# Ten more projection columns by seven block products, in a single-core hybrid decoder step

## What is computed

```python
h = rmsnorm(x, norm1_w)
proj = jnp.einsum('btd,de->bte', h, w_in)
u_pool, u_qkv, b_raw, a_raw, z, gate_pool, gate_delta = jnp.split(proj, SPLITS, axis=-1)
qkv, conv_buf_new = causal_conv(u_qkv, conv_buf, w_conv)
o, s_new = gated_delta_chunked(q, k, v, g, beta, s0, chunk)
o = rmsnorm(o, o_norm_w) * jax.nn.silu(z.reshape(B, T, N_HEADS, HEAD_DV).astype(f32))
merged = jax.nn.sigmoid(gate_pool) * branch_pool + jax.nn.sigmoid(gate_delta) * branch_delta
x = x + jnp.einsum('btd,de->bte', merged, w_out)
```

## Time and profile before

| | |
|---|---|
| median of 3 runs | 602.62 us (601.82 to 602.76) |
| the profiled execution | 602.27 us, its span 600.5 us |
| busy: PE, PEld | 548.7 us (91%), 409.4 us (68%) |
| busy: DVE, ACT, POOL | 270.1, 147.2, 135.2 us |
| HBM | 150.05 MB read, 263 GB/s over the span |

### The profile page before, as it was taken

How to read it: one execution, slowest core, us unless ns; L and a number is a source line. 1 busy time by engine, 2 the same in 40 slices (tenths; PEclk the granted TensorE clock), 3 DMA queues, 4 the chain that set the end, 5 groups by cost and what they waited for, 6 DMA issues and landing times.

```text
span 600.5 us, 12000 instructions
## 1 busy us (share of the span) xinstructions
PE 548.7 (91%) x4820; PEld 409.4 (68%) x4820; DVE 270.1 (45%) x754; ACT 147.2 (25%) x389; POOL 135.2 (23%) x228
## 2 busy tenths in 40 slices
PE   8999999999999999999999999999495959699873
PEld 7899999777877755578889888755262626266431
DVE  4567767755443426146546244651314040414125
ACT  3366465237720002033100133111010101010012
POOL 5777774121200540035004421200000000000000
PEclk9999999999999999999999999999789898999988
DMA  9755444839934273542378944999999999999982
GB/s 242 232 159 151 154 142 141 281 112 332 306 87 134 45 264 110 172 123 89 109 260 350 381 180 199 365 422 420 409 422 419 423 420 419 422 420 419 421 330 79
DMA packets 82582, 158.59 MB, mean 264 GB/s; under 512 B 11245, under 2 KB 65274, under 8 KB 70849
## 3 DMA queue, kind: packets, MB, share of 16 engines
q1 hardware_dynamic: 79724, 154.22, 70.1%
q10 hardware_dynamic: 2805, 3.62, 2.0%
HBM read 150.05 MB, written 7.96 MB: 263 GB/s over the span
## 4 chain that ended last, share of the span: by engine, by line
PE 72%; DMA 23%; DVE 2%; SPq 1%; issue 1%; ACT 1%; DVEq 0%; ACTq 0%
DMA arena<-in_w_up_dram 21%; PE ps L1360 21%; PE ps L1369 13%; PE ps L2013 8%; PE ps L1881 5%; PE ps L1830 3%; PE ps L1784 3%; PE ps L1313 2%; DMA arena<-in_w_in_dram 1%; SPq L582 1%; PE ps L1823 1%; PE ps L2088 1%; PE ps L2068 1%; PE ps L1566 1%; PE ps L1530 1%; PE ps L2025 1%
## 5 line engine op out<-in xcount | busy, mean ns | idle before, releaser
L1360 PE MATMUL ps<-arena 128*128 128x288 f32 x480 | 130.1, 416 | 1.2 <-DMA arena<-in_w_in_dram 1.2
L1360 PEld LDWEIGHTS ps<-arena 128*128 128x128 f32 x480 | 87.3, 190 | 26.8 <-issue 3.1
L2013 PE MATMUL ps<-arena 128*32 128x256 f32 x1024 | 69.3, 433 | 29.0 <-DMA arena<-in_w_up_dram 27.6
L2013 PEld LDWEIGHTS ps<-arena 128*32 128x32 f32 x1024 | 40.1, 124 | 56.7 <-issue 43.2
L1369 PE MATMUL ps<-arena 128*128 128x144 f32 x616 | 78.3, 288 | 0.0
L1369 PEld LDWEIGHTS ps<-arena 128*128 128x128 f32 x616 | 76.3, 190 | 2.5 <-issue 1.9
L2229 DVE SCALAR_TENSOR_TENSOR ps<-arena,ps 128x312 f32<-128x312 f32 x72 | 39.1, 545 | 2.4 <-ACT ps L1021 0.9
L2025 PE MATMUL ps<-arena 128*128 128x128 f32 x336 | 38.7, 276 | 0.0
L2025 PEld LDWEIGHTS ps<-arena 128*128 128x128 f32 x336 | 38.1, 192 | 0.4 <-DVE arena L2898 0.4
L2919 DVE TENSOR_TENSOR arena<-arena,ps 128x256 f32<-128x256 f32 x8 | 3.4, 421 | 66.8 <-issue 36.6
L2088 PE MATMUL ps<-arena 128*128 128x512 f32 x64 | 31.2, 618 | 1.9 <-ACT arena L1258 1.0
(11 more groups left out here) (410 smaller groups left out, 747.3 us busy)
## 6 DMA issues: line engine op xcount, KB each, us to landing
arena<-in_w_up_dram SPq DMA_DIRECT2D x32, 1024.0 KB, 17.3
arena<-in_w_gate_dram SPq DMA_DIRECT2D x28, 1024.0 KB, 18.1
arena<-in_w_down_dram SPq DMA_DIRECT2D x28, 1024.0 KB, 18.6
arena<-in_w_in_dram SPq DMA_DIRECT2D x26, 1024.0 KB, 6.7
out_dram<-arena SPq DMA_DIRECT2D x9, 512.0 KB, 7.6
arena<-in_w_branch_delta_dram SPq DMA_DIRECT2D x4, 1024.0 KB, 6.3
arena<-in_w_out_dram SPq DMA_DIRECT2D x4, 1024.0 KB, 5.4
arena<-in_w_gate_dram SPq DMA_DIRECT2D x8, 512.0 KB, 9.5
```

The lines of the kernel that those rows point to most:

```text
L1360: last = mm(ps[n % 2][:, 0:T], w[:, k, P * (n % 2):P * (n % 2) + P], hT[:, k, :], start=(k == 0), stop=(k == KD - 1))
L2013: last = mm(to[CAP * e:CAP * e + CAP, 0:FE], xgT[u][:, k, CAP * e:CAP * e + CAP], w[e][:, k, :], start=(k == 0), stop=(k == KD - 1))
```

## The change

Items 15 to 19 (z2 to z7, g0 to g3) now go by `fast_pair` too, with banks 0, 1, 3 and 4 (heads keep 5 and 6, samples 7 and 2). Pool makes five more sets of weight sums: those of item 15 ahead of its wait for the convolutions and ahead of the row masks, 16 and 17 ahead of its wait for the zero image's transfer, 18 and 19 around `own_columns`. The slots of items 12 to 23 change from a ring of six to one of four, as slots 4 and 5 hold sums. The heads' buffers `Dt` and `egq` get a second copy each, and a head's decays are made ahead. PE makes one head inside each of the first four pairs and one behind. ACT copies the first product, and applies silu or tanh in three pieces per pair.

```diff
-FAST = range(1, NQKV // 2)
+QKV_FAST = range(1, NQKV // 2)
+Z_FAST = range(15, 20)
+FAST = [*QKV_FAST, *Z_FAST]
-SLOT_OF = [i % 4 if i < NQKV // 2 else i % RA for i in range(A_ITEMS)]
+SLOT_OF = [i % 4 if i < 24 else i % RA for i in range(A_ITEMS)]
...
-DIAG_AT = (N_GATE + 2) // 2 + RA - 1
+DIAG_AT = (N_GATE + 2) // 2 + 3
...
+            sum_weights(15)
             pool.wait_ge(S["conv"], NQKV)
             pool.wait_ge(S["wp_pe"], NG)
...
             nc.gpsimd.memset(XT, 0.0).then_inc(S["memsets"], 1)
+            sum_weights(16)
+            sum_weights(17)
             pool.wait_ge(S["diag"], 16)
             own_columns(0)
+            sum_weights(18)
             pool.wait_ge(S["sd_pe"], 1)
             own_columns(1)
+            sum_weights(19)
...
+            for i in Z_FAST:
+                h = 2 * (i - Z_FAST[0])
+                if 0 < h < H:
+                    rows_exp(h)
+                first_of_pair(i)
+                if h == 0:
+                    rows_exp(0)
+                if h < H:
+                    rows_exp(h + 1)
...
+                pair_curves(i)
...
             pe.wait_ge(S["silu"], 3 * NQKV)
-            for h in range(H):
-                proj(N_Z + Z_AHEAD + h)
-                prep(h)
+            pe.wait_ge(S["wp_ev"], NG)
+
+            def between_pairs(i):
+
+                h = 2 * (i - Z_FAST[0])
+                if h < H:
+                    prep(h)
+                if h == 4:
+                    sample_tiles(2, 0, TS, Nq, lambda own, j: ident[own, own])
+                if h == 6:
+                    sample_tiles(4, 0, TS, IAq, lambda own, j: N2q[own, j, :])
+                if h == H:
+                    state_products(1)
+
+            for i in Z_FAST:
+                h = 2 * (i - Z_FAST[0])
+                fast_pair(i, lambda: between_pairs(i), (ps[0], ps[1], ps[3], ps[4]))
+                if h < H:
+                    prep(h + 1)
...
+            for n in range(2 * Z_FAST[-1] + 2, N_GATE + LEAD_GATES):
                 proj(n)
-                if n == N_GATE + 3:
+                if n == N_GATE + 4:
                     sample_tiles(7, 0, P, TTq, lambda own, j: Rq[own, j, :])
-                if n == N_GATE + 4:
+                if n == N_GATE + 5:
                     sample_tiles(8, 2 * P, P, aqq, lambda own, j: vnq[own, j, :])
```

The additions on DVE (`pair_u2`, `pair_u4`, `pair_u7`, `pair_u5`, `pair_u6`) have this form, and stand among the heads as the third piece of the order below shows:

```diff
+            def pair_u7(i):
+                d0, d1 = pair_rows(i)
+                dve.wait_ge(S["proj"], product(i, P7))
+                dve.wait_ge(S["sums"], added(i, SUM4))
+                V.tensor_tensor(d1[:, HT:T], d1[:, HT:T], ps[4][:, 0:HT], ALU.add).then_inc(S["sums"], 1)
```

More of the change, by code:

```diff
@@ L259, in hybrid_step @@
         kq, vnq = quads(wk.take(2 * P)), quads(wk.take(2 * P))
+        Dts, egqs = (Dt, wk.take(TP)), (egq, wk.take(P))
         vx = rb_room4.rearrange("p (b e) -> p b e", b=BD)
@@ L410, in hybrid_step @@
         for n in range(N_PROJ):
[L411 removed]
+            free[n] = (free[n - 1] if n else 0) + ((3 if n % 2 else 1) if n // 2 in Z_FAST else 1 if n // 2 in FAST else 2 if n < N_POOL else 3 if n < N_Z else 1)
         def chunk(n):
@@ L775, in _ @@
             old_columns(1)
-            for i in FAST:
+            for i in QKV_FAST:
                 raw_copy(2 * i - 2)
@@ L1084, in _, with first_of_pair, curve, pair_curves @@
                 pool_rows(2 * n + 1)
-            for h in range(H):
-                rows_exp(h)
-                if h == 1:
+            def first_of_pair(i):
+                d0, d1 = pair_rows(i)
+                act.wait_ge(S["proj"], product(i, P1))
+                nc.scalar.activation(d0[:, HT:T], ps[0][:, 0:HT], ACT.Copy).then_inc(S["proj_free"], 1)
+            def curve(to, src, i):
+                if 2 * i < N_GATE:
+                    nc.scalar.activation(to, src, ACT.Silu).then_inc(S["proj_free"], 1)
+                else:
+                    nc.scalar.activation(to, src, ACT.Tanh, scale=0.5).then_inc(S["proj_free"], 1)
+            def pair_curves(i):
+                d0, d1 = pair_rows(i)
+                act.wait_ge(S["proj"], product(i, P2))
+                curve(d0[:, 0:HT], ps[0][:, 0:HT], i)
+                act.wait_ge(S["sums"], added(i, SUM5))
+                curve(d0[:, HT:T], d0[:, HT:T], i)
+                act.wait_ge(S["sums"], added(i, SUM6))
+                curve(d1, d1, i)
+            for i in Z_FAST:
[7 more added lines that the diff above has]
+                    rows_exp(h + 1)
+                if h == 2:
                     act.wait_ge(S["decdve"], 1)
                     nc.scalar.activation(Dq, Dq, ACT.Exp).then_inc(S["dec_act"], 1)
-                evac(N_Z + Z_AHEAD + h)
-            evac(N_Z + Z_AHEAD + H)
-            for n in range(N_GATE + 3, N_GATE + LEAD_GATES):
+                pair_curves(i)
+            for n in range(2 * Z_FAST[-1] + 2, N_GATE + LEAD_GATES):
                 evac(n)
@@ L1354, in proj @@
                 if n >= 2:
-                    pe.wait_ge(S["proj_free"], free[n - 2 if item - 1 not in FAST else 2 * item - 1])
+                    pe.wait_ge(S["proj_free"], free[n - 2] if item - 1 not in FAST else free[2 * item - 2] + 1)
                 w = slots[SLOT_OF[item]].rearrange("p (k n) -> p k n", k=KD)
@@ L1371, in block_product, with fast_pair @@
                 last.then_inc(S["proj"], 1)
-            def fast_pair(i, between):
+            def fast_pair(i, between, banks=(ps[0], ps[1], ps[4], ps[5])):
                 w = slots[SLOT_OF[i]].rearrange("p (k n) -> p k n", k=KD)
@@ L1504, in rows_flip @@
                 pe.wait_ge(S["by_token"], 1)
-                pe.wait_ge(S["sums"], added(FAST[-1], SUM6))
+                pe.wait_ge(S["sums"], added(QKV_FAST[-1], SUM6))
                 for c in range(2):
@@ L2524, in _ @@
             dve.wait_ge(S["wp_pe"], NG)
-            for h in range(H):
-                prep(h)
-                if h == 0:
-                    sample_decay()
-                if h == 1:
+            decays_of(0)
+            decays_of(1)
+            for i in Z_FAST:
+                h = 2 * (i - Z_FAST[0])
+                if h > 0:
+                    prep(h - 1)
+                if 0 < h < H:
+                    decays_of(h + 1)
+                if h == 2:
+                    sample_decay()
+                if h == 6:
+                    sample_inverse(1)
+                if h == H:
+                    sample_keys()
+                pair_u2(i)
+                pair_u4(i)
+                if 0 < h < H:
+                    betas_of(h)
+                    prep(h)
+                pair_u7(i)
+                if 0 < h < H:
+                    betas_of(h + 1)
+                pair_u5(i)
+                pair_u6(i)
+                if h == 0:
+                    betas_of(0)
+                    prep(0)
+                    betas_of(1)
+                if h + 2 < H:
+                    decays_of(h + 2)
+                if h == 2:
                     sample_masked()
-                if 2 <= h <= 4:
-                    sample_inverse(h - 2)
-                if h == 5:
-                    sample_keys()
+                if h == 4:
+                    sample_inverse(0)
+                if h == 6:
+                    sample_inverse(2)
             sample_values()
```

98 lines of the change are left out of this document (60 added, 38 removed).

## The result

The changed kernel takes 604.18 us (median of 20 runs, 602.03 to 609.61) where the kernel before takes 602.14 (20 runs beside them, 600.83 to 603.73): a ratio of 1.0046 as recorded, 95% interval 1.0031 to 1.0061 (the medians alone give 1.0034; all ratios below are the recorded ones). On two further chips the ratio was 1.0067 (1.0043 to 1.0091) and 1.0058 (1.0037 to 1.0079). One of the 17 runs of the kernel before on the second chip took 1395.68 us, counts as slow and is in no ratio. I had forecast 601.5, 0.95 us less than before on the profiled execution's path, range 599.7 to 603.8. The profiled execution took 602.81 with a span of 601.1 us.

What follows compares the result with a forecast made beforehand. PE was taken to bound the kernel; it saves 3.75 us, but the small product comes 1.6 us later and X holds PE, leaving a 0.95 us gain: 602.27 to 601.3, taken as 601.5, range 599.7 to 603.8.

Steps and rivals of the forecast that it cites:

- Pair 16, 0 to 0.3, taken as 0.15: PE's wait for U7 ahead of pair 16's last product: 8.45 us of DVE work against 8.6 on PE.
- What the other engines do for nothing: Pool's 20 further sums (25 us) and DVE's 25 additions (7.5 us) fit in idle time, at no cost.
- My sign of being wrong: Gaps above 0.3 us ahead of the last four matmuls of pairs 16 and 17 would show late U7.
- the second one: U7 late behind whole heads on DVE, its operations 20% longer: 3 us more stall, 604.3; chance 0.17.
- What PE saves: Weight loads from z2 to g8: 6.85 us a pair against 7.60 for two chunks, 3.75 us for five pairs.
- The start, +1.0: PE waits 1.0 us for the last `pool_mix` to be copied before item 15's first block product.
- The flips, +0.4: Before `sample_flips`, the samples' last inverse step stands on DVE behind U6 of the fourth pair: 0.4 us.
- The product's place and the fixed chain: Small product after g4, +0.05 us ahead of it; from it to X 19.68 us fixed; PE waits 1.2 us.
- rival 3: Gate g10's weights late behind the diagonal blocks' transfers: 2.0 us to spare or a wait of 1.2, 602.7; chance 0.04.
- The drain: About 1.38 us added to each ACT table load by the skill's rule: 601.8 instead of 601.5; chance 0.04.
- PE busy without a break: From 133 to 263 us PE is never idle, so time taken off it there is worth its full length.

Runs made afterwards that it cites:

- tiny sums: Changed kernel with Pool's twenty sum operations of the five new pairs cut from 128x512 to 128x4 (output differs): 601.40 us, ratio 1.0002.
- pieces: Changed kernel with each of Pool's twenty sums made as four operations of 128x128: 602.09 us, ratio 1.0004.
- updates first: Changed kernel with VectorE's order alone changed, U2 and U4 ahead of the decays, U7 ahead of the betas: 602.58 us, ratio 1.0010.
- last two pairs: Changed kernel with only items 18 and 19 as fast pairs, items 15 to 17 as plain chunks again: 602.39 us, ratio 1.0010.
- early product: Changed kernel with the samples' small product ahead of gate g4 and its needed values ahead of the last pair's U7: 602.32 us, ratio 1.0011.
- tiny sums, early product: Changed kernel with Pool's additions cut to 4 columns (stale sums) and the small product moved ahead of g4: 597.46 us, ratio 0.9921.
- pieces, early product: Changed kernel with Pool's sums in four operations each and the small product moved ahead of g4: 599.56 us, ratio 0.9971.
- its three variants: Kernel before with sixteen Pool additions, copies or clears of 128x384 put beside the first heads: 604.74, 601.38 and 602.13 us, one run each.
- the kernel made to bring it on: Changed kernel with three VectorE additions of 128x96 ahead of update U2 of item 16: 606.01 us, ratio 1.0072.

## Why the prediction was wrong

| from the last `pool_mix`, us | small product | inner tiles | state products | ratio |
|---|---|---|---|---|
| before | 57.96 | 80.35 | 85.55 | 1 |
| changed | 62.28 | 81.89 | 87.85 | 1.0046 |
| tiny sums | 58.29 | 77.80 | 84.68 | 1.0002 |
| pieces | 59.10 | 78.53 | 85.43 | 1.0004 |
| updates first | 59.80 | 79.36 | 85.52 | 1.0010 |
| last two pairs | 61.37 | 80.92 | 86.13 | 1.0010 |
| early product | 58.14 | 80.53 | 85.73 | 1.0011 |
| tiny sums, early product | 54.31 | 76.69 | 81.90 | 0.9921 |
| pieces, early product | 55.18 | 77.57 | 82.78 | 0.9971 |

Each row is one profiled run and a ratio of 6 to 20 runs. The two agree to about 1 us: pieces with the early product has the state products 2.77 us sooner and takes some 1.8 us less, and tiny sums has them 0.87 us sooner and takes no less. What takes the rest, later in the kernel, stays open.

- **The step that failed** is "Pair 16, 0 to 0.3, taken as 0.15", with "What the other engines do for nothing" behind it. I had five operations of 256 columns at 0.45 us; beside Pool's sums such operations take up to 1.50. Without that contention the tiles come 4.1 us sooner (tiny sums against changed) or 3.8 us (the same two with the early product). The term was 0.15. My sign of being wrong, gaps above 0.3 us ahead of the last four matmuls of pairs 16 and 17, is there: 0.73 and 0.75.
- **The rival that came true in its mechanism is the second one**: U7 late behind whole heads on VectorE, PE's waits in items 16 and 17. I priced it at 604.3 and gave it 0.17. That this lies near the measured 604.18 is in part luck: its two waits, 1.6 and about 1, are 2.45 us more than my 0.15 and not 3, which by its own path gives some 603.7; and it had nothing for the loss behind the tiles. What I held against it, that additions and sums ran side by side in the q, k, v part, was no evidence: L2268 reads one input from PSUM, and the runs here show such operations unstretched. "20% longer" was the wrong form too. An operation isn't slowed by a share, it stands for the rest of Pool's instruction: 1.50, 1.49 and 1.38 us, each ending 0.27 to 0.29 behind it.
- **What PE saves** was sized a little low. With its two heads (0.86 and 0.96 us up to the next start) taken off, pair 15 with tiny sums takes 6.94 us (134.34 to 143.10), and the two plain chunks in the version with the last two pairs take 7.83 us (134.73 to 144.38), 0.89 us saved where I had 0.75.
- **The start, +1.0**: the gap is there, a little smaller. From the last `pool_mix` to the first product behind it it is 1.85 us in every version, 1.05 before (132.21 to 133.26), so 0.8. It isn't the block product's doing: the version with the last two pairs, whose item 15 is a plain chunk, has it too. It belongs to the wait for the copies, which now stands ahead of the chunk.
- **The flips, +0.4**: no such gap in any profile. With the sums tiny, the small product came 0.33 us later than before, where my terms without pair 16's gave 1.45; the 0.7 us that I had missed in the saving, the 0.4 of the flips and the 0.2 that the start had too much make 1.3, a little more than the difference of 1.1.
- **The product's place and the fixed chain** were right: 19.59 us against 19.68, and a wait of 1.03 against 1.2. Since the product was 2.7 us later than forecast, X came later by the same, and a gain of 0.95 us at the tiles became a loss of 1.54. Both causes had to go for a gain: without the gaps alone, 1.0002; without the wait alone, 1.0011.
- **Behind the tiles** I had nothing. The changed kernel loses another 0.76 us up to the state products, where its trace shows a wait of 0.69 us for nothing visible. Such a wait, 0.61 to 1.62 us, is in seven of the eight profiles in which PE waited for X at the tiles (not in that with the last two pairs), and absent in the eight where PE didn't, the kernel before with its three variants and the four versions with the early product. What it is stays open. No load came late ahead of g10 (rival 3): PE took it up straight behind the state products.
- **The drain** that I had weighed against the change does not show either: in the changed kernel a table load of 1.28 us starts at 139.48 and ScalarE's next operation at 140.77. **PE busy without a break** up to 263 us was not quite so: the earlier trace rows has 49.75 of 50.50 us from 212.5 on. Nothing hung on it.
- **Open**: the runs of 606 us and more, 8 of 20 on the first chip. Their mean granted clock over the whole run is 0.963 to 0.971, in seven of the eight 0.969 or below, where the other 12 have 0.970 to 0.974. So the long runs spend more time at the lower clock, but where, and whether the gaps bring it on, isn't shown; a low mean alone doesn't make a long run (pieces with the early product has four at 0.967 that took 598.88 to 599.45). One profile of such a run shows the fall of the granted clock, 1.6 us, but the kernel made to bring it on didn't show it. None of the versions without the gaps or with the early product had a run above 605.6. The granted clock also changes in the last third of every profile, the kernel before included, and I can't divide the rest between these.

## What to carry to other kernels

An engine's idle share says nothing on whether another engine's work beside it is free: before moving elementwise work to Pool, list the VectorE operations that will run beside it with all their inputs in SBUF, and allow each one the length of a Pool instruction. A cover of 0.15 us on the path of the busiest engine is then no cover. Where it can't be avoided, cut Pool's instructions short (20 of 1.3 us did harm, 80 of 0.49 hardly any, though they took longer in all), or let VectorE first do what TensorE waits for (the new order left no block product waiting, with Pool's sums unchanged). And where a chain of fixed length leads from an early product to a late consumer, saving work behind that product alone brings only the slack: move the product up in the same edit.

## What I had not expected of the hardware

- A VectorE operation with both inputs in SBUF (128x256 float32, 0.42 us) that begins while Pool adds from SBUF ends 0.27 to 0.29 us behind Pool's instruction: six of them take 1.27 to 1.50 us in the changed kernel's profile. Pool gives way a little too, 1.27 us becoming 1.32 to 1.45 where the two meet. Beside Pool copies it took up to 0.72 us, beside Pool clears 0.43, and operations with one input in PSUM were not stretched in the profiles read here.
- The size of the stalls differs from run to run: 2.46, 2.76 and 3.55 us of gaps in three profiles of one kernel. Its times spread wider too, 602.03 to 609.61 where the kernel before has 600.83 to 603.73, with 20 runs each; that the stalls alone do this isn't shown, since the version with pieces, with gaps of 0.19 and 0.17 us, still spreads from 600.04 to 605.56.
